# A two-block transformer on one core: the rotary key joined with the gate inputs in one projection, constant products and work moved in the routers

## What is computed

```python
def even_mixer(x, w_in, ...):
    h = x @ w_in                                  # 1024 x 1952
    c_q, c_kv, k_pe, gq, gk, gv, g_lr, gr = _split(h, (256, 128, 32, 256, 256, 512, 32, 512))
    k_pe = apply_rope(k_pe, cos_a, sin_a)         # 32 rows, shared by the 8 heads
    ...
    lr_f, lr_b = g_lr[..., :16], g_lr[..., 16:]
    la_f = log_sigmoid(lr_f @ gla_gate_w_fwd + gla_gate_b_fwd) / 16
    la_b = log_sigmoid(lr_b @ gla_gate_w_bwd + gla_gate_b_bwd) / 16
    ...                                           # gated linear attention in both directions

def expert_choice_moe(x, router_w, w1, w3, w2):
    aff = softmax(x @ router_w)                   # 256 x 16
    gates, idx = top_k(aff.T, 32)
    ...
```

## Time and profile before

| what | value |
|---|---|
| median of 3 runs (lowest, highest) | 2194.75 us (2192.29, 2197.65) |
| the profiled execution, its own time | 2190.09 us |
| its span, first to last instruction | 2188.3 us |
| TensorE busy | 1778.1 us (81%) |
| VectorE busy, ScalarE busy | 445.4 us (20%), 396.9 us (18%) |
| mean granted TensorE clock | 0.896 of 2.4 GHz |
| read from memory | 826.16 MB, 378 GB/s over the span |

### The profile page before, as it was taken

One profiled execution on the slowest core, in us unless ns is written; L12 is line 12 of the kernel. 1 busy time (PEld: TensorE's weight loads), 2 busy tenths in 40 slices (PEclk: granted clock), 3 DMA queues, 4 the chain that ended last, 5 costly groups with the idle time before them and its releaser, 6 DMA issues.

```text
span 2188.3 us, 31075 instructions
## 1 busy us (share of the span) xinstructions
PE 1778.1 (81%) x13285; PEld 1112.9 (51%) x13285; DVE 445.4 (20%) x1063; ACT 396.9 (18%) x907; POOL 0.6 (0%) x5
## 2 busy tenths in 40 slices
PE   7989999899999988998987565656789975756657
PEld 5868665568576655686844121211577641212214
DVE  3242211123633111225211000000234310000002
ACT  3131311122623111234211000000223210000001
POOL 0000000000000000000000000000000000000000
PEclk9999999999999999999999787787999998786878
DMA  9867899986647999843499999999933799999996
GB/s 358 276 252 266 324 394 394 383 241 229 220 147 313 364 395 396 300 135 135 173 351 420 421 421 422 421 422 421 351 136 112 280 413 421 421 421 421 421 422 273
DMA packets 185024, 716.00 MB, mean 327 GB/s; under 512 B 28428, under 2 KB 95928, under 8 KB 114360
## 3 DMA queue, kind: packets, MB, share of 16 engines
q1 hardware_dynamic: 184172, 713.48, 83.5%
q10 hardware_dynamic: 716, 0.53, 0.1%
HBM read 826.16 MB, written 1.05 MB: 378 GB/s over the span
## 4 chain that ended last, share of the span: by engine, by line
PE 57%; DMA 34%; DVE 4%; SPq 2%; ACT 1%; issue 1%; DVEq 0%; ACTq 0%
DMA ring<-in_w 27%; PE ps L1002 19%; PE ps L1429 7%; PE ps L1352 7%; DMA ring<-in_moe_w_up 5%; PE ps L1362 3%; PE ps L1470 3%; PE ps L1380 3%; PE ps L1336 2%; PE ps L979 2%; PE ps L1144 2%; SPq L823 1%; DMA ring<-in_ada_w 1%; PE ps L1071 1%; PE ps L1186 1%
## 5 line engine op out<-in xcount | busy, mean ns | idle before, releaser
L1429 PE MATMUL ps<-ring,ptb 128*32 128x512 f32 x1936 | 318.8, 809 | 204.4 <-DMA ring<-in_w 190.7
L1429 PEld LDWEIGHTS ps<-ring,ptb 128*32 128x32 f32 x1936 | 84.1, 142 | 426.3 <-issue 410.9
L1470 PE MATMUL ps<-ring,pb 128*32 128x512 f32 x1024 | 141.7, 708 | 73.8 <-DMA ring<-in_w 72.5
L1002 PE MATMUL ps<-xT,ring 128*128 128x256 f32 (+2 forms) x640 | 145.0, 385 | 1.0 <-ACT xT L1758 0.4
L1002 PEld LDWEIGHTS ps<-xT,ring 128*128 128x128 f32 (+2 forms) x640 | 116.5, 185 | 29.0 <-issue 8.6
L1470 PEld LDWEIGHTS ps<-ring,pb 128*32 128x32 f32 x1024 | 37.9, 127 | 170.3 <-issue 167.7
L2531 DVE TENSOR_TENSOR kT<-pb,ps 128x1024 f32<-128x1024 f32 x8 | 9.8, 1221 | 536.2 <-ACT pb L1948 536.2
L1002 PE MATMUL ps<-oT,ring 128*128 128x256 f32 x512 | 114.0, 381 | 2.0 <-DVE oT L2288 1.1
L1002 PE MATMUL ps<-hT,ring 128*128 128x256 f32 x480 | 106.3, 384 | 1.3 <-ACT hT L1758 1.3
L1352 PE MATMUL ps<-ring,vt 128*32 128x256 f32 x1536 | 92.6, 400 | 15.4 <-DMA ring<-in_moe_w_up 13.6
L1002 PEld LDWEIGHTS ps<-oT,ring 128*128 128x128 f32 x512 | 96.2, 190 | 15.6 <-DVE oT L2288 2.0
(11 more groups left out here) (463 smaller groups left out, 1945.4 us busy)
## 6 DMA issues: line engine op xcount, KB each, us to landing
ring<-in_w SPq DMA_DIRECT2D x370, 1024.0 KB
ring<-in_moe_w_gate SPq DMA_DIRECT2D x96, 1024.0 KB
ring<-in_moe_w_up SPq DMA_DIRECT2D x96, 1024.0 KB
ring<-in_moe_w_down SPq DMA_DIRECT2D x96, 1024.0 KB
ring<-in_ada_w SPq DMA_DIRECT2D x48, 1024.0 KB
ring<-in_diff_w_in SPq DMA_DIRECT2D x12, 1024.0 KB
ring<-in_w_o SPq DMA_DIRECT2D x8, 1024.0 KB
ring<-in_ple_gate_w SPq DMA_DIRECT2D x8, 1024.0 KB
```

Of the source, the lines that this page charges most:

```text
L1002: last = mmul(o, l, r, start=start, stop=stop)
L1429: last = mmul(ps[32 * j:32 * j + 32, 2 * a + h, :], xg[:, k, 32 * j:32 * j + 32], w[j][2 * k2 + h], start=(k == 0), stop=(k == C - 1))
L1470: last = mmul(ps[32 * j:32 * j + 32, 6 + h, :], hidT2[:, c, 32 * j:32 * j + 32], w[j][2 * c2 + h], start=(c == 0), stop=(c == C - 1))
```

## The change

Four parts. (a) `ev_kpe` is gone: its 32 columns ride in the slot and job of `ev_lr`, whose 24 products now go chunk by chunk to three column positions (partitions 0, 32 and 64). The slot is filled by two transfers, the second with its own semaphore `kpe_in`. `kpe` lies in `st`, and `ev_ckv` and `ev_cq` change places. (b) The gate products carry their bias in a seventeenth row: VectorE writes ones into `rt` before the gate inputs are copied there, the bias is loaded as row 17 of the gate weights, and the two directions lie at partitions 0 and 32. Eight products become four. (c) `route1` does all of `ada_part` before the selection, then four constant products, one between the sums and the comparison, and five at the end. `route2` projects its third value job behind the transposes of the affinities, evacuates no value job ahead of the exponentials, and has two and two constant products. (d) `experts2` turns the first group's combine weights and spreads the deviations after the first sixteen products of `gate_up(0)`.

```diff
-        kpe = scr[:, 768:1024]
+        kpe = st[:, :]
...
-        lrT = rt[0:16, 0:512].rearrange("p (a t) -> p a t", a=2)
+        lr_rows = [rt[32 * d:32 * d + 17, 0:T] for d in range(2)]
+        gate_rows = [gwb[32 * d:32 * d + 17, 0, :] for d in range(2)]
...
-        ev_lr = job(ew[:, 1440:1472], 8, 32, mm_T(xT, 8, [(0, 16, 0, 0), (16, 16, 0, T)]),
-                    copy_to((lambda b: ps[0:16, b, :], rt[0:16, 0:512])), need=("h_ready", 5))
+        def lr_kpe(w, bank):
+            return [[(ps[r0:r0 + m, bank, 0:T], w[:, kk, c0:c0 + m], xT[:, kk, :], kk == 0, kk == C - 1)
+                     for kk in range(C) for c0, m, r0 in ((32, 16, 0), (48, 16, 32), (0, 32, 64))]]
+        ev_lr = job(ew[:, 1440:1472], 8, 64, lr_kpe,
+                    copy_to(*[(lambda b, d=d: ps[32 * d:32 * d + 16, b, 0:T], rt[32 * d:32 * d + 16, 0:T]) for d in range(2)],
+                            (lambda b: ps[64:96, b, 0:T], kpe[64:96, :])), need=("h_ready", 5))
...
-        ev_kpe = job(ew[:, 384:416], 8, 32, mm_T(xT, 8, [(0, 32, 64, 0)]),
-                     copy_to((lambda b: ps[64:96, b, 0:T], kpe[64:96, :])))
...
+                        if j == ev_lr:
+                            load(jb["slot"], dst[:, :, 32:64], src)
+                            sp.dma_start(dst[:, :, 0:32], ew[:, 384:416].rearrange("(k p) n -> p k n", p=P))\
+                                .then_inc(S("kpe_in"), 16)
...
             def route1(m):
-                ada = ADA_FIRST + ADA_ROUTER[m], ps[:, 0, 0:T]
-                ada_part(*ada, range(0, 4))
+                ada_part(ADA_FIRST + ADA_ROUTER[m], ps[:, 0, 0:T])
+                idle_products(1, 4)
...
                 rank_of(sel, E1, m).then_inc(S("rank_mm"), 1)
-                ada_part(*ada, range(4, 6))
                 pe.wait_ge(S("blocks_ready"), 2 * m + 1)
...
-                ada_part(*ada, range(6, 8))
+                idle_products(1, 1)
                 pe.wait_ge(S("blocks_ready"), 2 * m + 2)
...
                 ada_columns([ADA_ROUTER[m]], (5,))
-                idle_products(1, 4)
+                idle_products(1, 5)
...
             def route2(m):
-                values = list(span[f"value{m - 2}"])
-                project(values[2:3])
                 pe.wait_ge(S("aff_ready"), m - 1)
...
-                project(values[3:])
-                idle_products(4, 4)
+                project(span[f"value{m - 2}"][2:])
+                idle_products(4, 2)
...
-                idle_products(4, 1)
+                idle_products(4, 2)
...
+                def turn_weights(i):
+                    pe.wait_ge(S("DA_ready"), E2_GROUPS * l + i + 1)
+                    for tt in range(TT):
+                        last = tr(ps[:, 6, P * tt:P * tt + P], DAg[:, tt, :])
+                    last.then_inc(S("C_mm"), 1)
+                def spread_deviations():
+                    for tt in range(TT):
+                        for a, x in enumerate((rstd, away)):
+                            last = mmul(ps[:, 7, T * a + P * tt:T * a + P * tt + P],
+                                        x[:, tt:tt + 1].to_broadcast([P, P]), ident, start=True, stop=True)
+                    last.then_inc(S("rstd_mm"), 1)
                 def gate_up(i):
...
+                            if i == 0 and s == 0:
+                                turn_weights(0)
+                                spread_deviations()
...
             def gla_gates():
-                for d in range(2):
-                    for tt in range(TT):
-                        mmul(ps[:, 4 + d, T * tt:T * tt + T], lrT[:, d, P * tt:P * tt + P], gw[:, d, :],
-                             start=True, stop=False)
-                        last = mmul(ps[:, 4 + d, T * tt:T * tt + T], K("ones", 1), rows1[0:1, GB0 + T * d:GB0 + T * d + T],
-                                    start=False, stop=True)
+                for tt in range(TT):
+                    for d in range(2):
+                        last = mmul(ps[:, 4 + d, T * tt:T * tt + T], lr_rows[d][:, P * tt:P * tt + P], gate_rows[d],
+                                    start=True, stop=True)
...
             gla_scores()
+            project([ev_ckv])
+            gla_updates()
             project([ev_cq])
-            gla_updates()
-            project([ev_ckv, ev_kpe])
             gla_outputs()
...
             def route2(m):                       # ScalarE
                 root(m)
-                evacuate(span[f"value{m - 2}"][0:1])
...
                 last.then_inc(S("sum_ready"), 1)
-                evacuate(span[f"value{m - 2}"][1:3])
+                evacuate(span[f"value{m - 2}"][0:2])
                 tokens(m, 0)
                 tokens(m, 1)
-                evacuate(span[f"value{m - 2}"][3:])
+                evacuate(span[f"value{m - 2}"][2:])
...
             experts1(1)
+            V.memset(rt[0:64, 0:T], 1.0).then_inc(S("ones_rows"), 1)
             norm(4)
```

More of the change, by code:

```diff
@@ L180, in program @@
         gwb = sb("gw", [P, 2, T])
-        gw = gwb[0:16, :, :]
         cpad = sb("cpad", [P, C, 32])
@@ L277, in col @@
             return colsA[parts, 1, R1[name][0] + k:R1[name][0] + k + 1]
-        LAM0, GB0, RB0 = 0, 256, 768
+        LAM0, RB0 = 0, 768
         def slot_view(n, k, cols):
@@ L464, in program @@
                               gv[:, :, 256 * s:256 * s + 256]))) for s in range(2)]
+        ev_ckv = job(ew[:, 256:384], 8, 128, mm_T(xT, 8, [(0, P, 0, 0)]),
+                     copy_to((lambda b: ps[:, b, 0:T], ckvT[:, 0, :])))
         ev_cq = job(ew[:, 0:256], 8, 256, mm_T(xT, 8, [(0, P, 0, 0), (P, P, 0, T)]),
                     copy_to((whole, scr[:, 0:512])))
-        ev_ckv = job(ew[:, 256:384], 8, 128, mm_T(xT, 8, [(0, P, 0, 0)]),
-                     copy_to((lambda b: ps[:, b, 0:T], ckvT[:, 0, :])))
-        ev_kpe = job(ew[:, 384:416], 8, 32, mm_T(xT, 8, [(0, 32, 64, 0)]),
-                     copy_to((lambda b: ps[64:96, b, 0:T], kpe[64:96, :])))
         ev_gr = [job(ew[:, 1472 + 256 * s:1728 + 256 * s], 8, 256, mm_T(xT, 8, [(0, P, 0, 0), (P, P, 0, T)]),
@@ L638, in program @@
         r_even = len(ropes)
-        ropes.append((kpe, 1, 64, 32, SWAP_32, K("cos_m"), K("sin_m"), ("job", ev_kpe)))
+        ropes.append((kpe, 1, 64, 32, SWAP_32, K("cos_m"), K("sin_m"), ("job", ev_lr)))
         for s in range(4):
@@ L838, in load_late @@
             def load_late():
-                late(rows1[0:1, GB0:GB0 + 256], A["gla_gate_b_fwd_2"])
-                late(rows1[0:1, GB0 + 256:GB0 + 512], A["gla_gate_b_bwd_2"])
                 for l in range(2):
@@ L852, in load_late @@
                     late(turned2[:, a, :, :], A[name].rearrange("l (q k) -> q l k", k=C))
-                late(gw[:, 0, :], A["gla_gate_w_fwd_2"][0])
-                late(gw[:, 1, :], A["gla_gate_w_bwd_2"][0])
+                for d, name in enumerate(("fwd", "bwd")):
+                    late(gate_rows[d][0:16, :], A[f"gla_gate_w_{name}_2"][0])
+                    late(gate_rows[d][16:17, :], A[f"gla_gate_b_{name}_2"])
                 assert n_late[0] == N_LATE, n_late
@@ L860, in load_jobs @@
                     if jb["new"]:
-                        load(jb["slot"], slot_view(jb["slot"], jb["k"], jb["cols"]),
-                             jb["W"].rearrange("(k p) n -> p k n", p=P))
+                        dst, src = slot_view(jb["slot"], jb["k"], jb["cols"]), jb["W"].rearrange("(k p) n -> p k n", p=P)
+                        if j == ev_lr:
+                            load(jb["slot"], dst[:, :, 32:64], src)
+                            sp.dma_start(dst[:, :, 0:32], ew[:, 384:416].rearrange("(k p) n -> p k n", p=P))\
+                                .then_inc(S("kpe_in"), 16)
+                        else:
+                            load(jb["slot"], dst, src)
             def load_experts1(m):
@@ L998, in project @@
                             if chunked and x == 0:
-                                name, value = h_chunk(jb["need"][1] - 1, i)
+                                name, value = h_chunk(jb["need"][1] - 1, C * i // len(grp))
                                 pe.wait_ge(S(name), value)
@@ L1135, in norm_router, with ada_part @@
                 project(fill[0:2])
-            def ada_part(p, dst, chunks=range(C)):
-                for k in chunks:
+            def ada_part(p, dst):
+                for k in range(C):
                     n = ada_slot(p, k // 2)
@@ L1480, in experts2 @@
                     n = E2_GROUPS * l + i + 1
-                    pe.wait_ge(S("DA_ready"), n)
-                    for tt in range(TT):
-                        last = tr(ps[:, 6, P * tt:P * tt + P], DAg[:, tt, :])
-                    last.then_inc(S("C_mm"), 1)
-                    if i == 0:
-                        for tt in range(TT):
-                            for a, x in enumerate((rstd, away)):
-                                last = mmul(ps[:, 7, T * a + P * tt:T * a + P * tt + P],
```

(10 more changed lines are left out.)

1 line of the change is left out of this document (removed).

## The result

| what | before | after |
|---|---|---|
| median (lowest, highest) | 2194.85 us (2192.29, 2197.65) | 2168.39 us (2164.29, 2172.57) |
| ratio, 95% interval | | 0.9873 [0.9856, 0.9889] |
| the profiled execution | 2190.09 us | 2167.44 us |
| TensorE busy | 1778.1 us | 1768.7 us |
| mean granted TensorE clock | 0.896 | 0.902 |

26.5 us faster by the medians, 22.65 by the two profiled executions. The forecast was 19.25. By time the result is at the low edge of the range (2168 to 2184), and nearest to the rival in which the clock stays up everywhere (2170.4).

A forecast was written before the change was run, and what follows sets the result against it. TensorE and the weight stream were taken to bound alternating stages, expert stages shifting with their first products. 5.7 + 6.95 + 2.5 + 4.1 = 19.25 us off the 2194.75 median gave 2175.5 us, range 2168 to 2184.

The forecast's parts named there:

- the clock stays up everywhere: Rival: TensorE's clock holds in all routers, `route2` too, gathers about 1 us shorter per layer; gain 24.4, 2170.4 us; chance 0.17.
- Part 1: First block's two routers: reordered `ada_part` and constant products save 5.7 us, the middle between 8.5 (fast clock) and 2.9 (slow).
- Part 5: Second block's routers and expert starts: 0.86 us sooner at the selection, 1.19 at `gate_up(0)`; 4.1 us for both layers.
- What bounds the kernel: TensorE and weight stream alternate; expert stages shift with their first products, so a microsecond saved ahead is one at the end.
- the upper bound of 3.5: First block's first router: the saving from selection to gather if the clock stays at 2.4 GHz, 3.5 us.
- Part 2: Mixer's gate inputs and key part in one job: 24 products side by side at three column positions, 6.95 us saved.
- Part 3: Mixer's gates: four products instead of eight, two directions alternating, 1.2 us in place of 3.66; 2.5 us saved.
- Part 4: Mixer's swapped order, `ev_ckv` between scores and updates in place of `ev_cq`: costs nothing if covered, 2.1 us without cover.
- rival E: Experiment's rival, second mixture: the stream alone sets these stretches, slower when started sooner; stage keeps 250 us, 2168.4; no chance given.
- the key part's load holds up the queue: Slower case, mixer: the key part's load, now second transfer in 1024 pieces of 128 bytes, delays loads; 2199 or more; chance 0.02.
- the columns run in a row: Rival, mixer's joined job: its 24 products run one after the other; gain 12.3, 2182.5 us; chance 0.06.
- the first mixtures swallow their routers' gain: Rival, first block's expert stages: something else starts their stream, so router savings vanish; gain 13.55, 2181.2 us; chance 0.04.

The follow-up runs named there:

- same_again: The changed kernel run again, unaltered; 2170.25 us, 0.9885 of the kernel before.
- old_gates: Changed kernel with the gates' bias as its own products again, eight instead of four, direction by direction, directions still at partitions 0 and 32; 2172.6 us.
- old_order_filled: Changed kernel with the second block's routers in their order of before, but six and two constant products in place of four and one; 2168.56 us.
- cq_first: Changed kernel with `ev_cq` and `ev_ckv` swapped back, jobs and calls; 2172.01 us, 0.9893 of the kernel before.
- the filled stalls: Changed kernel with seven constant products ahead of the up-projection weight wait in seven groups of the first block's two mixtures; 2167.31 us.

## Why the prediction was right or wrong

**The step that failed** is what the clock does behind short gaps, in two terms of the sum: the middle that Part 1 takes between the two levels, and the gather of `route2`, which Part 5 leaves at its length of before. The edited stretches save 24.3 us by the rows where the sum has 19.25: 7.6 for 5.7, 9.8 for 9.45 (Parts 2 and 3), 6.9 for 4.1.

**What bounds the kernel** was right. An expert stage shifts with its first products: the lead at the first `gate_up` of the first `experts2` (19.84) and that of the second (22.70) are kept to the end, and 8.6 us of added products come out as 6.4 to 8.3 us, by the changed kernel's two medians.

**Part 1, the routers: 5.7 forecast, 7.6 in the rows.** This step failed in size. "Between the two I take the middle" was wrong for the first router, where the clock held and the upper bound of 3.5 was passed (3.75), and half right for the second, where it fell and came back (3.87 of 5.0). In `same_again` it held in both, for 3.76 and 5.20, 9.0 together; in the six profiles in which the second fell for longer that router still saves 3.6, since the clock falls some 2 to 3 us behind the selection and not at it. The lower bound (2.2) had it slow throughout. The sums' start came as worked out, and so did the end of the constant products where the clock held. The 4.60 us that Part 1 gives as TensorE's idle time is that of the weight loads; its matmuls stood 4.12, and 0.47 now.

**Part 2, the joined job: 6.95 forecast, 7.2 in the rows** (3.4 on `ev_lr`, 3.6 for `ev_kpe` with its hand-over, 0.2 in small pieces). The row of four column positions was the right one to go by.

**Part 3, the gates: 2.5 forecast, 2.59 in the rows.** The size was right, but not the mechanism: I had put it on two directions alternating, and the order makes no difference. What counts is that four products are left (1.83) and, by `old_gates`, that the directions lie at different rows (0.76).

**Part 4, the swap, at nothing:** right (57.74 and 57.75).

**Part 5: 4.1 forecast, 6.9 in the rows.** The second step that failed in size, and for the same cause. 2.3 of the difference is the gather, 3.81 in place of 5.14 and 4.82: the gather of `route2` before, with its clock of 0.69, was carried over to a kernel whose gap in that place is 0.34 and not 1.21. I had read the gap there as "short"; with it filled the clock holds (`old_order_filled`). The order alone gives 1.1 at the selection, for 0.86 forecast, and 1.1 at the expert start, for 1.19.

**What was not in the sum at all.** The second mixture gave back 4.2 us and stretches that nobody edited gave 3.5. Both are differences of single executions: the first selection comes between 219.2 and 223.6 us in the profiles of kernels that are the same up to there, and the second mixture takes 243.8 to 251.4. Of the mixture the rows point to the clock behind its stalls, but the filled stalls leave rival E open; the cause of the 3.5 us stays open. The step from the profile's 22.65 to the medians' 26.5 is made of the same: the profiled execution of before lay 4.76 us under its median, that of after 0.95. So of the 7.2 us between 19.25 and 26.5, 5.1 are the mis-sized terms, 3.8 this step, and the stretches outside the edits take off 1.6.

**The rivals.** The clock up everywhere, given 0.17, came closest. Its working (8.5 for the routers of the first block and 2 for the gathers, where 2.3 was measured) is what `same_again` shows in rows; in the changed kernel's own profile the second router fell short of it, so that the agreement of the whole, 24.4 and 24.3, is in part luck. By the Trainium skill ("TensorE: Matmul & The Clock Gate", Part 1), where activity lifts the slow default and idle gaps bring it back, the products hold the clock. The trace agrees in the first router and in both second-block routers, with 1.00 throughout; in the second router it does not, since the clock falls behind gaps of 0.47 and 0.20 us with constant products on either side. The same part of the Trainium skill says that the point of the change varies from run to run; in the second router that is so of the fall, with 2.32 us for its ten records in `same_again` and `old_order_filled` and 4.01 in `old_gates` and `cq_first`, all with the same router code. That the key part's load holds up the queue, that the columns run in a row, and that the first mixtures swallow their routers' gain as a rule did not come true.

## What to carry to other kernels

Before you drop or move filler work, look at the gap that it leaves on TensorE and at the clock of the windows behind it: three products of 0.43 us, two of them in a gap of 1.2 us, were worth 1.2 to 1.3 us in the gather behind, in each layer. A wait for weights is such a gap too: constant products ahead of it kept the 64 records behind it at 3.66 us in every place where they were put. That this shortens the whole kernel is not shown. And products over few columns belong at different column positions with neighbours that alternate: the joined job took 3.6 us that way and 8.8 group by group.

## What was not expected of the hardware

- Behind a stall of 3.3 to 4.6 us the clock can be down for 64 records (up to 6.44 us) or not at all (3.66), in executions of the same kernel; two of them differ by 2 us in that stage.
- Two sets of gate products at partitions 0 and 32 take 1.13 us for eight records in either order, less than the estimate of 1.72 for four such products one after the other.
- Twenty-four products of 16 or 32 columns in groups took 8.8 us, 0.37 each, where sixteen of 16 columns took 7.0 before, 0.44 each.
